# Modulation groups of a two-layer RWKV/attention step: from ten units with two each to all sixteen units

## What is computed

```
def modulation(cond, w_mod, b_mod):
    m = jax.nn.silu(cond) @ w_mod + b_mod
    return jnp.split(m, 6, axis=-1)

sh1, sc1, gt1, sh2, sc2, gt2 = modulation(cond_ctx, w_mod[l], b_mod[l])
h = rmsnorm(xp, g_pre_mix[l]) * (1.0 + sc1) + sh1
o, k_ctx, v_ctx, s_ctx = mix_context(h, lp)
xp = xp + gt1 * rmsnorm(o, g_post_mix[l])
```

## Time and profile before

| | |
|---|---|
| median of 3 runs | 2732.68 us (2728.0 to 2733.49) |
| the profiled execution | 2720.77 us |
| its span | 2719.0 us |
| TensorE (PE) matmul busy | 92% of the span, 30324 matmuls |
| VectorE (DVE) busy | 53% |
| ScalarE (ACT) busy | 39% |
| GpSimd (POOL) busy | 11% |
| weights and other loads from HBM | 273.11 MB, a mean of 110 GB/s read and written |

### The profile page before, as it was taken

The page is one execution under the profiler, slowest core; times in us unless marked ns, Lnnn a source line. Parts: engine busy times, 40 slices in busy tenths (PEclk is TensorE's granted clock), DMA queues, the critical chain, the costliest instruction groups (busy, mean ns, idle before and its releaser), DMA issues.

```text
span 2719.0 us, 67961 instructions
## 1 busy us (share of the span) xinstructions
PE 2492.1 (92%) x30324; PEld 2193.1 (81%) x30324; DVE 1449.9 (53%) x2522; ACT 1068.6 (39%) x1926; POOL 306.5 (11%) x307
## 2 busy tenths in 40 slices
PE   6998789988999999989987888888999999999996
PEld 3996577776798998969965767767999999999995
DVE  2337556666533333362375657665565555555565
ACT  3226433334421212242254334344444444444452
POOL 0002123330000000010011333301100000000011
PEclk8999899999999999989998999998999999999998
DMA  7223123200122222212200330002765666666572
GB/s 274 78 78 127 38 91 127 103 28 6 70 78 78 73 76 78 78 66 78 72 16 2 127 127 4 4 5 82 268 211 179 214 210 209 182 211 212 180 260 82
DMA packets 82700, 304.57 MB, mean 112 GB/s; under 512 B 9376, under 2 KB 9504, under 8 KB 82272
## 3 DMA queue, kind: packets, MB, share of 16 engines
q1 hardware_dynamic: 71072, 257.93, 28.8%
q0 software_dynamic: 11328, 42.21, 4.2%
HBM read 273.11 MB, written 27.00 MB: 110 GB/s over the span
## 4 chain that ended last, share of the span: by engine, by line
PE 81%; DVE 11%; issue 3%; ACT 3%; DMA 1%; POOL 1%; SPq 0%; DVEq 0%; ACTq 0%; POOLq 0%
PE ps L451 19%; PE ps L452 19%; PE ps L453 19%; PE ps L1181 6%; PE ps L464 2%; PE ps L915 2%; PE ps L810 1%; PE ps L958 1%; PE ps L1113 1%; PE ps L974 1%; DMA ring<-in_blocks 1%; PE ps L818 1%; DVE arena L2451 1%; DVE arena L2450 1%; PE ps L463 1%
## 5 line engine op out<-in xcount | busy, mean ns | idle before, releaser
L2258 DVE TENSOR_TENSOR ring_lo<-ring,w_ffn 128x1024 fp32r<-128x1024 f32 x264 | 322.4, 1225 | 214.4 <-ACT w_ffn L1700 208.7
L451 PE MATMUL ps<-hg_hi,w_ffn 128*128 128x256 f32 x1408 | 401.6, 285 | 0.9 <-DVE hg_lo L2891 0.9
L452 PE MATMUL ps<-hg_lo,w_ffn 128*128 128x256 f32 x1408 | 397.2, 282 | 0.0
L453 PE MATMUL ps<-hg_hi,ring_lo 128*128 128x256 f32 x1408 | 396.7, 282 | 0.0
L1700 ACT ACTIVATE w_ffn<-ring 128x1024 fp32r<-128x1024 f32 x264 | 278.2, 1057 | 197.8 <-PE ps L453 197.5
L451 PEld LDWEIGHTS ps<-hg_hi,w_ffn 128*128 128x128 f32 x1408 | 266.5, 189 | 2.6 <-DVE hg_lo L2891 1.1
L452 PEld LDWEIGHTS ps<-hg_lo,w_ffn 128*128 128x128 f32 x1408 | 265.6, 189 | 1.2
L453 PEld LDWEIGHTS ps<-hg_hi,ring_lo 128*128 128x128 f32 x1408 | 266.2, 189 | 0.0
L1181 PEld LDWEIGHTS ps<-arena 64*64 64x64 f32 x7680 | 168.8, 139 | 72.6 <-issue 63.1
L453 PE MATMUL ps<-hT_ffn_hi,ring_lo 128*128 128x320 f32 x704 | 215.5, 306 | 0.0
L451 PE MATMUL ps<-hT_hi,w_proj 128*128 128x320 f32 x672 | 205.7, 306 | 7.0 <-DVE hT_lo L2264 6.9
(11 more groups left out here) (379 smaller groups left out, 5205.0 us busy)
## 6 DMA issues: line engine op xcount, KB each, us to landing
ring<-in_blocks SPq DMA_DIRECT2D x484, 512.0 KB, 3.7
h_rows<-arena POOLq DMA_DIRECT2D x16, 512.0 KB, 10.2
arena<-h_rows POOLq DMA_DIRECT2D x7, 1024.0 KB, 11.1
y_rows<-arena POOLq DMA_DIRECT2D x7, 1024.0 KB, 6.6
x<-in_x_all SPq DMA_DIRECT2D x1, 2560.0 KB, 13.4
h_plain<-arena POOLq DMA_DIRECT2D x1, 2560.0 KB, 16.0
out_y_all<-x POOLq DMA_DIRECT2D x5, 512.0 KB, 3.6
w<-in_low POOLq DMA_DIRECT2D x2, 768.0 KB, 6.4
```

Source lines behind the costliest of these rows:

```text
L451: nc.tensor.matmul(dst, w_hi, m_hi, start=start, stop=False)
L452: nc.tensor.matmul(dst, w_hi, m_lo, start=False, stop=False)
L453: return nc.tensor.matmul(dst, w_lo, m_hi, start=False, stop=stop)
L2258: V.tensor_tensor(ring_lo[:, n % RING, :], ring[:, n % RING, :], high[:, n % high.shape[1], :], ALU.subtract).then_inc(*E.sig("w_lo"))
```

## The change

The rule for which group stands where is replaced. `mod_groups(g)` gives the list of groups of unit g (0 to 15 over both layers): in layer 0 two for even units and one for odd ones, in layer 1 one for each. `mod_slots(g)` gives for each of them the slots of its four blocks, of its row copy and of its turn and bias: with two groups ((4, 4, 5, 6), 7, 8) in bank 6 and ((6, 7, 8, 9), 10, 11) in bank 7, with one group ((4, 6, 8, 9), 10, 11) in bank 6. The waits before slot 4's blocks (`ta_ev`, `vt_ev`) and for the last bias at the unit's end are in every unit. The number and the order of blocks, rows and turns are the same.

```diff
--- before.py
+++ after.py
@@ -655,10 +655,6 @@
 
             return banks2(b0, b1, 2 * CH * len(half_tiles(b))).rearrange("p h (i a t) -> p h i a t", a=2, t=CH)
 
-        def mods_before(l, it):
-
-            return sum(mod_group(l * UNITS + i, j) is not None for i in range(max(0, it)) for j in range(2)) + (MOD_FIRST if l == 0 else MOD_MID)
-
         def diag(n):
             return diags[:, n % 4, :]
 
@@ -672,12 +668,18 @@
 
             return 4 * (m + 1) + (0 if m < MOD_FIRST else PROJ_B if m < MOD_MID else 2 * PROJ_B + WO_B + DENSE_B)
 
-        def mod_group(g, j):
-
-            if g < (MOD_MID - MOD_FIRST) // 2:
-                return MOD_FIRST + 2 * g + j
-            g -= 2 * NPAIR
-            return MOD_MID + 2 * g + j if 0 <= g < (2 * MOD_G - MOD_MID) // 2 else None
+        def mod_groups(g):
+
+            if g is None:
+                return []
+            if g < UNITS:
+                at = MOD_FIRST + 3 * (g // 2) + 2 * (g % 2)
+                return [at, at + 1] if g % 2 == 0 else [at]
+            return [MOD_MID + g - UNITS]
+
+        def mod_slots(g):
+
+            return [((4, 4, 5, 6), 7, 8), ((6, 7, 8, 9), 10, 11)] if len(mod_groups(g)) == 2 else [((4, 6, 8, 9), 10, 11)]
 
         def ahead(f):
 
@@ -1233,7 +1235,6 @@
             def rwkv_second(l, it):
 
                 a, b, n = unit_at(l, it), unit_at(l, it - 1), unit_at(l, it + 1)
-                m0 = mod_group(l * UNITS + it, 0) if a is not None else None
                 for s in range(1, 13):
                     if a is not None:
                         level_block(a, (s + 1) // 2, (s + 1) % 2)
@@ -1252,16 +1253,15 @@
                     if n is not None and n % 2 == 0 and s == 3:
                         pe.wait_ge(sem["ta_ev"], n + 1)
                         values(n)
-                    if m0 is not None:
-                        if s == 4:
-                            if n is not None:
-                                pe.wait_ge(sem["ta_ev"], n + 1)
-                                pe.wait_ge(sem["vt_ev"], n // 2 + 1)
-                        if 4 <= s <= 7:
-                            for q in range(2):
-                                mod_block(2 * (s % 2) + q, 6 if s < 6 else 7)
-                        if s in (7, 8):
-                            mod_turn(m0 + s - 7, s - 1)
+                    if a is not None and s == 4 and n is not None:
+                        pe.wait_ge(sem["ta_ev"], n + 1)
+                        pe.wait_ge(sem["vt_ev"], n // 2 + 1)
+                    for k, (m, (blocks_at, row_at, turn_at)) in enumerate(zip(mod_groups(a), mod_slots(a))):
+                        for q in range(4):
+                            if blocks_at[q] == s:
+                                mod_block(q, 6 + k)
+                        if turn_at == s:
+                            mod_turn(m, 6 + k)
                     if b is not None and s == 9:
                         pe.wait_ge(sem["sc_ev"], SCAN * (b + 1))
                         v, kr = vtk[:, (b // 2) % 2, :, :, :], kr_m[:, b % 2, :, :, :]
@@ -1288,8 +1288,8 @@
                                     mm = nc.tensor.matmul(ps[r, (4, 5)[p], chunk(i)], q_at(b % 2, j)[r, :], gq[r, j, :],
                                                           start=False, stop=i == NT - 1, skip_group_check=True)
                         mm.then_inc(sem["y_mm"], 1)
-                if m0 is not None:
-                    pe.wait_ge(sem["mod_ev"], m0 + 2)
+                if a is not None:
+                    pe.wait_ge(sem["mod_ev"], mod_groups(a)[-1] + 1)
 
             def rwkv_phase(l):
                 rwkv_start(l)
@@ -1942,8 +1941,9 @@
                             values_ev(n)
                         if s in (5, 6, 10):
                             exps(n, s, b)
-                    if m0 is not None and s in (5, 7):
-                        mod_row(m0 + (s - 5) // 2, 6 + (s - 5) // 2)
+                    for k, (m, (blocks_at, row_at, turn_at)) in enumerate(zip(mod_groups(a), mod_slots(a))):
+                        if row_at == s:
+                            mod_row(m, 6 + k)
                     if b is not None and b % 2 == 0 and s == 11:
                         c = (b // 2) % NPAIR
                         act.wait_ge(sem["y_mm"], b + 1)
@@ -2529,8 +2528,9 @@
                         gn_early(l, s)
                     if n is not None:
                         prep(l, n, s, a)
-                    if m0 is not None and s in (7, 8):
-                        mod_bias(m0 + s - 7, s - 1)
+                    for k, (m, (blocks_at, row_at, turn_at)) in enumerate(zip(mod_groups(a), mod_slots(a))):
+                        if turn_at == s:
+                            mod_bias(m, 6 + k)
                     if b is not None and b % 2 == 1 and s == 11:
                         y = by_parity(oT[:, 4 + (b // 2) % NPAIR, :].rearrange("p (j t) -> p j t", t=CH))
                         dve.wait_ge(sem["y_mm"], b + 1)
```

## The result

The changed kernel's median is 2736.28 us (2729.66 to 2744.03, 20 runs), that of the kernel before, run beside it on the same chip, 2727.9 us (2722.34 to 2736.33, 20 runs). The ratio is 1.0029 with a 95% interval of 1.0021 to 1.0037. The sign of the forecast was wrong; the time lies inside the range. The profiled execution took 2739.34 us.

A forecast was written before the change was run, and what follows sets the result against it. TensorE's order was taken as the bound (81% of the span), with free time in slots 4 to 7. Four two-group units at 5.7 plus twelve at 2.0 give 46.8 against 58 us: -11, median 2721.7 us, range 2703 to 2741.

The forecast's parts named there:

- A pair costs 5.8 us, which is 6.0 us of TensorE's order: RWKV units: a pair of groups adds 5.8 us, nearly all from blocks (4.0) and turns (1.96) on TensorE.
- Blocks in slots 4 and 6: 0.5 us each, hidden: One-group units: these blocks lie beside the VectorE and GpSimd chain with TensorE idle, so 0; uncovered 1.0 us.
- Slots 8 and 9: +0.4 and +0.5: One-group units: slot 8's block has 0.1 us of cover; slot 9's has none, TensorE being the chain.
- Turn in slot 11: +0.98 - 0.35: One-group units: the turn adds 0.98 us, less 0.35 averaged cover from VectorE's unit end in even units.
- fetch stops -0.55: Slots 9 to 12: slow blocks run into instruction-packet stops (0.56 and 0.60 us) at no cost, half taken as saved.
- Weight traffic +0.8 for a group: Loads released in slots 8 and 9 meet packet fetches: +0.8 us, bounds 0 and 2.2 plus 0.7 of clock.
- Units with two groups 5.7, last units 2.0: Price over an empty unit: two groups (even units, layer 0) 5.7 us; one group, last units included, 2.0 us.
- Copies, bias, waits: 0: Moved ScalarE row copy, slot 4's transpose wait and unit-end bias wait cost 0, the bias at most 0.2 us.
- The weights for the output projection after unit 7: 0: Output projection weights, queued after unit 7 instead of 5, still arrive before they are wanted: 0 us.
- B: Rival: the price goes with the work, a group costs 2.9 us wherever it stands; 0 us change, chance 0.24.
- C: Rival: weight traffic moves onto the instruction fetches of slots 9 to 12; +18 us, slower, chance 0.16.
- D: Rival: one group vanishes in the fetch stops, costing only 0.7 us; -30 us, chance 0.21.

The follow-up runs named there:

- e8: Changed kernel with each unit's first group in the old slots (paired blocks 4, 4, 5, 5, row 5, turn 7); 1.0007 against the kernel before.
- e13: e1 with each unit's last row and turn moved to slots 10 and 11 (first of two groups: 7 and 8); 1.0042 against the kernel before.
- e14: Changed kernel with only the last row and turn one slot earlier (9 and 10), blocks as late; 1.0000 against the kernel before.
- second execution: Kernel before and changed kernel, both unchanged, each profiled once more; 2724.06 and 2725.22 us, one execution each.
- e4: Kernel before with RWKV modulation blocks loaded at 32 of 1024 columns, matmuls on a constant; 4696.94 us with an overflow pass, RWKV units 559.8.
- e1: Changed kernel, groups still spread, but everything in slots 4 to 8 (one group: blocks 4, 5, 6, 7, turn 8); 0.9991 against the kernel before.
- e7: Changed kernel, still spread, with blocks early and in pairs (one group: 4, 4, 6, 6, row 7, turn 8); 1.0009 against the kernel before.
- e12: e1 with weight loads delayed until the next unit's gram products; 1.0035 against the kernel before.
- e11: e8 with weight loads delayed until the next unit's gram products; 1.0015 against the kernel before.
- e5: Kernel before with both blocks of a slot on the same two quarters, so they cannot run side by side; 1.0011 against the kernel before.
- e6: Changed kernel with blocks joined to pairs again, still late (one group: 4, 4, 9, 9, turn 11); 1.0059 against the kernel before.

## Why the prediction was wrong, step by step

Three steps failed. The prediction priced a lone block at half of a pair, 0.5 us, and it takes 0.98 to 1.05. It took the rest of a pair's price for TensorE's order, where the traffic was more than half, so spreading had less to win than the sum gave: e8, with paired blocks, gains nothing either. With both, the units stay where they were. And it priced the turn in slot 11 at 0.98 - 0.35 = 0.63 us; by the medians of e13 and e14 this place is what makes the kernel slower, and in e13 it costs 14.2 us over sixteen units, 0.9 each.

- *A pair costs 5.8 us, which is 6.0 us of TensorE's order.* The 5.8 was measured rightly (41.3 against 35.9 in the second execution), its reading was not. Without traffic a pair costs 2.6 us (e4); the rest goes with the traffic, with its stops and half clocks. That two sums agreed (6.0 and 5.8) was a coincidence, and it hid that the order was largely covered already.
- *Blocks in slots 4 and 6: 0.5 us each, hidden.* The duration failed: 0.98 to 1.05. The cover mostly held: in unit 13 slot 6's block is off the chain, slot 4's is on it ahead of VectorE's L2558. Slots 4 to 8 of units 9 to 14 take 10.42 us against 9.45 in units 12 to 14 of before: +1.0, where +0.4 was forecast for them. This is the step in which a unit with one group went over the working.
- *Slots 8 and 9: +0.4 and +0.5.* Both blocks are on the chain at 0.98. This is the same error, **half a pair's time for a lone block**, a price of the earlier trace rows divided by two without a row that shows one.
- *Turn in slot 11: +0.98 - 0.35; fetch stops -0.55.* The turn's own 1.0 was right for its slot (1.6 against 0.5 in e13, 1.55 to 1.65 in most units of the changed kernel). What I left out is what it does where it stood: in slot 8 it was covered by the wait for a packet (e1 and e13), so leaving it gains little. I applied "slow matmuls run into the stop at no cost" to the new place and not to the old. Slots 9 to 12 of units 9 to 14 cost 8.90 us against 7.54: +1.4, forecast +1.6 with the traffic in it. This sum came out near by luck, since it holds the block of slot 9 at half of its time; and the empty units vary (8.2 us in the second execution of before).
- *Weight traffic +0.8 for a group.* For a unit with one group this was right in size: 38.0 us against 37.3 without the traffic, 0.7. What was missed is how much of it stood in the old place: over all units it costs 26.5 us before and 19.1 after. The order lost more than this gain of 7.
- *Units with two groups 5.7, last units 2.0.* Measured 42.63 - 35.48 = 7.2 and 35.85 - 32.45 = 3.4 (6.1 and 3.0 in the second execution). With two groups the block matmuls now need 6 us (two pairs and four lone blocks) where four pairs needed 4; the working had counted eight halves.
- *Copies, bias, waits: 0.* The bias is not off the path: at the end of unit 10 the chain goes from the turn through VectorE's bias to L2538. The bias itself is 0.04 us there; what it passes on is the turn. No wait for a copy was found on the chains read.
- *The weights for the output projection after unit 7: 0.* Not 0, as far as two executions tell: 1.2 to 4.4 us at the end of layer 0's RWKV part.
- *Rivals.* B, "the price goes with the work, 0 us", has the RWKV part right in number: the units' sums are equal, and a single group costs about 2.5 us in four placements. It does not have the reason, since e13 shows that the price depends on the place. C had the sign and the wrong cause: the traffic costs less after the change, and in slots 9 to 12 of the nine units with one group no stop on the chain is over 1.53 us (1.67 in the second execution), where C needed over 2. In unit 6, with two groups, slot 8 takes 6.35, which may be C at work, but slot 10 of unit 5 took 6.06 in the kernel before. D, a group that vanishes, is refuted: 19.32 us for slots 4 to 12 of units 9 to 14 against 16.99 in the empty ones, +2.3 us.
- *The range.* C was priced at +18 us, which is 2751, but the range was ended at 2741; that the time of 2736.28 lies inside it says nothing for the working.
- *The page's rule against the rows.* The stops with no producer on the chains above last 0.40 to 4.20 us, and the kernel without the traffic is 26.5 us quicker over the units. The Trainium skill ("Runtime: NRT & Kernel Launch", Instruction fetch mechanics) calls the crossing into a new block mostly hidden; these stretches of short matmuls do not agree.

What stays open: the 8.4 us of the medians are not split into places. The profiles show nothing for the units (means 587.3 before and 586.5 after), 1 to 4 us for the end of layer 0 and 4 to 5 us for the start, whose code is the same, within a spread of executions of some 4 us. That moving the turn and its row out of slots 11 and 10 removes the loss is shown by the medians of e14, and that putting them there makes one by e13; how much of it passes through stops and how much through the clock (e13 runs 38 us of its units at half clock, e1 20) is not. Why spreading the pairs (e7, e8) gains nothing is shown only as far as the price of a group, and why e12 loses 0.35% where e11 loses 0.15% was not followed up.

## What to carry to other kernels

Before an edit divides a group of instructions, look whether the group ran side by side: the price of one part has to come from a row that shows one part, not from the whole divided. Ask of a moved piece what covered it where it stood, with the same care as what covers it where it goes; a stop of the instruction stream covers work ahead of it as well as a data wait does (e1 against e13). And look what the moved piece's consumer holds up in its own queue: here VectorE's bias, and behind it the copy at the unit's end. When the sum of the pieces equals a measured difference, take away one cause (here the traffic) before believing it.

## What the runs showed of the hardware

- Two calls of one block on two quarters of TensorE's columns take 0.98 to 1.05 us, four calls of two blocks on four quarters 0.99 to 1.07; with both blocks on the same two quarters the line's time goes from 43.65 to 76.41 us (e5). The Trainium skill ("TensorEngine Tiling (Array Packing)", Key Properties) says that different tiles can load weights and multiply in parallel; the runs agree.
- In the trace's DMA records (e1, e13) an instruction packet's fetch begins 1.1 to 1.2 us after the packet before it is entered when no bulk load runs, and 2 to 4 us after when weight blocks are moving. Where TensorE stops for packets, their fetches are then 5.0 to 6.5 us apart instead of 3.5 to 3.8. Taking the bulk loads from 57 to 19 GB/s (layer 1, the rows beside e4) is worth 26.5 us of 586 over both layers.
- Kernels whose blocks run in pairs over all units had the lower clock: half clock for 61 to 68 us of the units in e6 to e8, 37 before, 11 in the changed kernel with its lone blocks, 20 in e5, where only the pairing of the kernel before is gone. Lone blocks alone do not decide it: 41 in e12 and 38 in e13.
